# The modulation vector as row sums on VectorE, over a matrix laid out transposed

## What is computed

```python
c_act = jax.nn.silu(c)                       # (1, 2048)
mod = c_act @ w_ada + b_ada                  # w_ada (2048, 6144)
shift, scale, gate = jnp.split(mod, 3, axis=-1)
h = rms_norm(x, g) * (1.0 + scale[:, None]) + shift[:, None]
...
return x + gate[:, None] * out
```

## Time and profile before

| | |
|---|---|
| median of three runs | 2671.77 us (2671.35 to 2673.11) |
| the profiled execution | 2669.51 us |
| its span, first to last instruction | 2668.2 us |
| mean granted clock of TensorE over the span | 0.998 of full |
| busy: TensorE, VectorE, ScalarE, GpSimd | 99%, 48%, 33%, 3% |
| HBM read, mean rate | 297.80 MB, 115 GB/s over the span |

### The profile page before, as it was taken

One profiled execution on the slowest core, in us unless ns is written; L12 is line 12 of the kernel. 1 busy time (PEld: TensorE's weight loads), 2 busy tenths in 40 slices (PEclk: granted clock), 3 DMA queues, 4 the chain that ended last, 5 costly groups with the idle time before them and its releaser, 6 DMA issues.

```text
span 2668.2 us, 28964 instructions
## 1 busy us (share of the span) xinstructions
PE 2631.1 (99%) x11830; PEld 2135.4 (80%) x11830; DVE 1276.1 (48%) x1806; ACT 888.8 (33%) x1232; POOL 91.9 (3%) x75
## 2 busy tenths in 40 slices
PE   8999999999999999999999999999999999999998
PEld 6888888888888888888888887778866777777888
DVE  7546634447434555655542263563343334443425
ACT  5633324333323222222232352332232333433323
POOL 4000000000000000000000011100000000000000
PEclk9999999999999999999999999999999999999999
DMA  5322233222233666666443223234312322222424
GB/s 180 103 80 71 79 87 99 84 79 71 87 95 123 209 209 209 201 204 211 142 158 110 88 87 107 83 100 162 95 54 65 95 71 79 72 72 86 160 100 150
DMA packets 159364, 308.07 MB, mean 115 GB/s; under 512 B 10944, under 2 KB 15296, under 8 KB 158208
## 3 DMA queue, kind: packets, MB, share of 16 engines
q1 hardware_dynamic: 158432, 304.65, 35.8%
q0 software_dynamic: 224, 1.15, 0.1%
q10 hardware_dynamic: 576, 0.43, 0.1%
HBM read 297.80 MB, written 8.39 MB: 115 GB/s over the span
## 4 chain that ended last, share of the span: by engine, by line
PE 93%; DVE 3%; issue 2%; ACT 1%; DMA 0%; POOL 0%; SPq 0%; ACTq 0%; DVEq 0%; POOLq 0%
PE bank L329 84%; PE bank L669 2%; PE bank L1205 1%; PE bank L1101 1%; PE bank L1179 1%; PE bank L385 1%; PE bank L688 1%; DVE WL L361 1%; DVE XL L454 1%; PE bank L1194 1%; PE bank L1090 1%; DMA X<-in_xT 0%; PE bank L956 0%; ACT WH L347 0%; DVE Y L1916 0%
## 5 line engine op out<-in xcount | busy, mean ns | idle before, releaser
L329 PE MATMUL bank<-XH,WH 128*128 128x512 f32 (+1 forms) x2880 | 1150.5, 399 | 19.0 <-DVE XL L454 10.6
L329 PE MATMUL bank<-XH,WL 128*128 128x512 f32 (+1 forms) x2880 | 1111.2, 386 | 3.8 <-DVE WL L361 3.8
L329 PE MATMUL bank<-XL,WH 128*128 128x512 f32 (+1 forms) x2880 | 1108.9, 385 | 0.0
L361 DVE TENSOR_TENSOR WL<-RAW,WH 128x1024 fp32r<-128x1024 f32 x444 | 547.7, 1236 | 960.7 <-ACT WH L347 959.9
L347 ACT CAST WH<-RAW 128x1024 fp32r<-128x1024 f32 x444 | 464.2, 1047 | 1202.8 <-PE bank L329 1197.1
L329 PEld LDWEIGHTS bank<-XH,WH 128*128 128x128 f32 x2880 | 542.5, 188 | 139.9 <-issue 31.8
L329 PEld LDWEIGHTS bank<-XL,WH 128*128 128x128 f32 x2880 | 542.8, 188 | 118.4 <-issue 15.8
L329 PEld LDWEIGHTS bank<-XH,WL 128*128 128x128 f32 x2880 | 542.0, 188 | 116.8 <-DVE WL L361 5.5
L329 PE MATMUL bank<-WH,XH 128*128 128x512 f32 x384 | 154.2, 401 | 0.0
L329 PE MATMUL bank<-WL,XH 128*128 128x512 f32 x384 | 149.6, 390 | 0.0
L329 PE MATMUL bank<-WH,XL 128*128 128x512 f32 x384 | 149.4, 389 | 0.0
(11 more groups left out here) (241 smaller groups left out, 1679.8 us busy)
## 6 DMA issues: line engine op xcount, KB each, us to landing
RAW<-in_w_in SPq DMA_DIRECT2D x304, 512.0 KB, 3.6
AST<-in_w_ada SPq DMA_DIRECT2D x192, 256.0 KB, 3.7
RAW<-in_w_out SPq DMA_DIRECT2D x40, 512.0 KB, 3.5
RAW<-in_w_o SPq DMA_DIRECT2D x32, 512.0 KB, 3.6
RAW<-in_w_gate SPq DMA_DIRECT2D x32, 512.0 KB, 3.6
RAW<-in_w_a SPq DMA_DIRECT2D x16, 512.0 KB, 4.1
RAW<-in_w_b SPq DMA_DIRECT2D x16, 512.0 KB, 4.1
XT<-in_xT SPq DMA_DIRECT2D x4, 1024.0 KB, 6.6
```

Source lines behind the costliest of these rows:

```text
L329: ins = nc.tensor.matmul(bank[b][:, cols], l, r[:, cols], start=first, stop=final)
L361: nc.vector.tensor_tensor(WL[:, m % NSPL], RAW[:, m % NRAW], WH[:, m % NSPL].bitcast(F32), ALU.subtract).then_inc(lo.sem, lo.step(m))
```

## The change

The matrix is handed over in another layout, made on the host: instead of 2048 rows (inputs) by 6144 columns (outputs) it is cut into 192 tiles of 128 outputs by 512 inputs, each contiguous. Tile n has the quarter q = n // 48 of the inputs and the block t = n % 48 of the outputs. Now an output lies on a partition, and its sum runs along the row. `c` comes as a row of 2048 numbers, of which 512 at a time are loaded to all 128 partitions (`load_c`, 256 KB in SBUF) into CB, two buffers; ScalarE makes its sigmoid in SGT (which lies where MASK was, used by the recurrence only), VectorE the product, silu(c), in CB.

For each tile VectorE then runs one `tensor_tensor_reduce`: the product of the tile and CB, written over the tile, and its row sums in one column of PART. After 192 tiles four small adds of 128x48 put together the four quarters and the bias into MOD. TensorE has no part in it; no PSUM bank is taken. The turns, their pace, the three tile buffers and the place in the order stay. The rows of c for quarter q + 1 are loaded at tile 8 of quarter q, their sigmoid is made at tile 24, their product at tile 32. The first is loaded ahead of the first three tiles.

```diff
@@ -264,7 +264,7 @@
     raw = [Signal(nc, f"raw{i}", 16) for i in range(NRAW)]
     ld = {name: Signal(nc, f"load_{name}", 16) for name in
           ("vec", "log", "idn", "msk", "x0", "x1", "x3", "x6", "x10", "xt0", "xt1", "xt2", "xt3", "p", "cst",
-           "ada0", "ada1", "ada2", "x3_0", "x3_1", "x3_2", "x3_3")}
+           "ada0", "ada1", "ada2", "c", "x3_0", "x3_1", "x3_2", "x3_3")}
     stored = Signal(nc, "out_stored", 16)
     spilled = Signal(nc, "x3_spilled", 16)
 
@@ -827,8 +827,9 @@
     M = sb("M", [16, 512], F32, W0 + 49152)
     SG = sb("SG", [4, 512], F32, W0 + 81920)
     AST = sb("AST", [3, 512], F32, W0 + 90112)
-    ACC = sb("ACC", [2, 512], F32, W0 + 96256)
-    CA = SM[:, 48:64]
+    CB = sb("CB", [2, 512], F32, W0 + 96256)
+    PART = sb("PART", [192], F32, W0 + 100352)
+    SGT = sb("SGT", [512], F32, C0 + 1024)
 
     def conv_dve(half):
         for i in range(4):
@@ -890,74 +891,72 @@
     O_MADE = [(dve, ("silu", ("og", j // 4), j % 4)) for j in range(8)]
     M_MADE = [(dve, ("m", j)) for j in range(16)]
 
+    def load_c(q):
+        nc.sync.dma_start(CB[:, q % 2], crow[:, 512 * q:512 * q + 512].partition_broadcast(128)
+                          ).then_inc(ld["c"].sem, ld["c"].step(q))
+
+    def load_ada(n):
+        s = ld[f"ada{n % 3}"]
+        nc.sync.dma_start(AST[:, n % 3], w_ada[n]).then_inc(s.sem, s.step(n))
+
     def ada_sp():
+        Y.wait_ge(xlo, (yield xlo, ("ya", 7)))
+        Y.wait_ge(dve, (yield dve, ("silu", ("og", 1), 3)))
+        load_c(0)
         for n in range(3):
-            if n == 0:
-                Y.wait_ge(xlo, (yield xlo, ("ya", 7)))
-                Y.wait_ge(dve, (yield dve, ("silu", ("og", 1), 3)))
             load_ada(n)
         yield
         for n in range(192):
+            q, t = divmod(n, 48)
             if n + 3 < 192:
                 Y.wait_ge(dve, (yield dve, ("ada", n)))
                 load_ada(n + 3)
-            yield
-
-    def load_ada(n):
-        c, k = divmod(n, 16)
-        s = ld[f"ada{n % 3}"]
-        nc.sync.dma_start(AST[:, n % 3], w_ada[k * 128:k * 128 + 128, 512 * c:512 * c + 512]
-                          ).then_inc(s.sem, s.step(n))
+            if t == 8 and q < 3:
+                load_c(q + 1)
+            yield
+
+    def c_act(q):
+        A.wait_ge(ld["c"], (yield ld["c"], q))
+        if q:
+            A.wait_ge(dve, (yield dve, ("c", q - 1)))
+        else:
+            A.wait_ge(dve, (yield dve, ("silu", ("og", 1), 3)))
+        A.use(SIG)
+        nc.scalar.activation(SGT[:, :], CB[:, q % 2], ACT.Sigmoid).then_inc(act.sem, act.step(("c", q)))
 
     def ada_act():
-        A.wait_ge(ld["vec"], (yield ld["vec"], 0))
-        A.use(SIG)
-        nc.scalar.activation(CA, vall("c"), ACT.Sigmoid).then_inc(act.sem, act.step("ca"))
-        yield
-        yield from idle(192)
+        yield from c_act(0)
+        yield
+        for n in range(192):
+            q, t = divmod(n, 48)
+            if t == 24 and q < 3:
+                yield from c_act(q + 1)
+            yield
+
+    def c_dve(q):
+        V.wait_ge(act, (yield act, ("c", q)))
+        nc.vector.tensor_tensor(CB[:, q % 2], CB[:, q % 2], SGT[:, :], ALU.mult).then_inc(dve.sem, dve.step(("c", q)))
 
     def ada_dve():
-        V.wait_ge(act, (yield act, "ca"))
-        nc.vector.tensor_tensor(CA, CA, vall("c"), ALU.mult).then_inc(dve.sem, dve.step("ca"))
+        yield from c_dve(0)
         yield
         for n in range(192):
-            c, k = divmod(n, 16)
-            s, u = n % 3, c % 2
-            V.wait_ge(ld[f"ada{s}"], (yield ld[f"ada{s}"], n))
-            if k == 0:
-                V.wait_ge(dve, (yield dve, "ca"))
-                if c > 1:
-                    V.wait_ge(side, (yield side, ("ada", c - 2)))
-                elif c == 0:
-                    V.wait_ge(dve, (yield dve, ("silu", ("og", 1), 3)))
-                nc.vector.tensor_scalar(ACC[:, u], AST[:, s], CA[:, 0:1], None, ALU.mult
-                                        ).then_inc(dve.sem, dve.step(("ada", n)))
-            else:
-                V.wait_ge(dve, (yield dve, ("ada", n - 1)))
-                nc.vector.scalar_tensor_tensor(out=ACC[:, u], in0=AST[:, s], scalar=CA[:, k:k + 1],
-                                               in1=ACC[:, u], op0=ALU.mult, op1=ALU.add
-                                               ).then_inc(dve.sem, dve.step(("ada", n)))
-            yield
-            if k == 15:
-                V.wait_ge(side, (yield side, ("ada", c)))
-                nc.vector.tensor_tensor(MOD[:, 4 * c:4 * c + 4], bank[banks["ada", c]][:, 0:4],
-                                        vall("b_ada")[:, 4 * c:4 * c + 4], ALU.add
-                                        ).then_inc(dve.sem, dve.step(("mod", c)))
-
-    def ada_pe():
-        yield
-        for n in range(192):
-            c, k = divmod(n, 16)
-            if k == 15:
-                b, was = special_bank(("ada", c), dve, ("mod", c))
-                T.wait_ge(was[0], (yield was))
-                T.wait_ge(dve, (yield dve, ("ada", n)))
-                for j in range(4):
-                    ins = nc.tensor.matmul(b[:, j:j + 1], ACC[:, c % 2, 128 * j:128 * j + 128], ONES[:, 0:1],
-                                           start=True, stop=True)
-                    if j == 3:
-                        ins.then_inc(side.sem, side.step(("ada", c)))
-            yield
+            q, t = divmod(n, 48)
+            if t == 32 and q < 3:
+                yield from c_dve(q + 1)
+            V.wait_ge(ld[f"ada{n % 3}"], (yield ld[f"ada{n % 3}"], n))
+            V.wait_ge(dve, (yield dve, ("c", q)))
+            nc.vector.tensor_tensor_reduce(AST[:, n % 3], AST[:, n % 3], CB[:, q % 2], 1.0, 0.0, ALU.mult, ALU.add,
+                                           PART[:, n:n + 1]).then_inc(dve.sem, dve.step(("ada", n)))
+            yield
+        V.wait_ge(dve, (yield dve, ("ada", 191)))
+        nc.vector.tensor_tensor(MOD[:, :], PART[:, 0:48], PART[:, 48:96], ALU.add).then_inc(dve.sem, dve.step("mod1"))
+        for q in (2, 3):
+            V.wait_ge(dve, (yield dve, f"mod{q - 1}"))
+            nc.vector.tensor_tensor(MOD[:, :], MOD[:, :], PART[:, 48 * q:48 * q + 48], ALU.add
+                                    ).then_inc(dve.sem, dve.step(f"mod{q}"))
+        V.wait_ge(dve, (yield dve, "mod3"))
+        nc.vector.tensor_tensor(MOD[:, :], MOD[:, :], vall("b_ada"), ALU.add).then_inc(dve.sem, dve.step("mod"))
 
     XT = sb("XT", [16, 512], F32, W0 + 49152)
     X1 = sb("X1", [16, 512], F32, W0)
@@ -1007,7 +1006,7 @@
                 yield
 
     def feed_h2_act():
-        A.wait_ge(dve, (yield dve, ("mod", 11)))
+        A.wait_ge(dve, (yield dve, "mod"))
         for k in range(16):
             A.wait_ge(dve, (yield dve, ("h2n", k)))
             A.wait_ge(dense, (yield dense, (("gate", 3), 3)))
@@ -1352,7 +1351,6 @@
         for g in range(4):
             yield from pe_dense(("ga", g), XH, XL, "h")
             if g == 0:
-                turns.specials.append(ada_pe())
                 turns.pace = 1.2
             yield from pe_dense(("wa", g), YH, YL, "ya")
         for g in range(4):
@@ -1871,7 +1869,7 @@
                     nc.vector.tensor_scalar(WG[:, i], WG[:, i], EPS, None, ALU.add
                                             ).then_inc(dve.sem, dve.step(*(["wg"] if i == 3 else [])))
         yield from rsqrt_dve("r_12", 1.0 / D, NN[:, 0], R12, NN[:, 2], eps=EPS * EPS)
-        V.wait_ge(dve, (yield dve, ("mod", 11)))
+        V.wait_ge(dve, (yield dve, "mod"))
         nc.vector.tensor_scalar(GG, MOD[:, 16:32], 1.0, None, ALU.add).then_inc(dve.sem, dve.step("gg0"))
         V.wait_ge(dve, (yield dve, "gg0"))
         nc.vector.tensor_tensor(GG, GG, vall("ng"), ALU.mult).then_inc(dve.sem, dve.step("gg"))
@@ -2082,7 +2080,8 @@
         "xT": np.ascontiguousarray(i["x"][0].T), "pT": np.ascontiguousarray(i["p"][0, 0].T),
         "vec": vec, "logits": logits, "cst": cst, "masks": masks, "ident": ident,
         "w_in": i["w_in"][0], "w_a": i["w_a_out"][0], "w_b": i["w_b_out"][0], "w_o": i["w_o"][0],
-        "w_gate": i["w_ple_gate"][0], "w_proj": i["w_ple_proj"][0], "w_ada": i["w_ada_2"][0],
+        "w_gate": i["w_ple_gate"][0], "w_proj": i["w_ple_proj"][0], "w_ada": i["w_ada_2"][0].reshape(4, 512, 48, 128).transpose(0, 2, 3, 1).reshape(192, 128, 512),
+        "crow": i["c_2"].reshape(1, D),
         "w_in2": i["w_in_2"][0], "w_out2": i["w_out_2"][0],
     }
     arrays = {f"in_{k}": np.ascontiguousarray(v) for k, v in arrays.items()}
```

More of the change, by code:

```diff
@@ L217, in build @@
 def build(nc, xT, pT, vec, logits, cst, masks, ident, w_in, w_a, w_b, w_o, w_gate, w_proj,
-          w_ada, w_in2, w_out2, out):
+          w_ada, crow, w_in2, w_out2, out):
     weights = {"w_in": w_in, "w_a": w_a, "w_b": w_b, "w_o": w_o, "w_gate": w_gate, "w_proj": w_proj,
@@ L919, in ada_dve @@
-    def ada_dve():
-        V.wait_ge(act, (yield act, "ca"))
```

(18 more changed lines are left out.)

## The result

The changed kernel takes 2658.42 us (median of four runs, 2657.58 to 2659.36) against 2671.86 before: a ratio of 0.9949, 95% interval 0.9938 to 0.9961, so 13.4 us (10.4 to 16.6) less. Forecast were 2659.5 us and 12.2 us less. The profiled execution took 2657.58, with a span of 2656.1; the sum had 2656.0.

A forecast was written before the change was run, and what follows sets the result against it. TensorE's dense products were taken to bound the stage; removing twelve small-product groups (11 x 0.90 + 2.34 = 12.2 us), with VectorE's work costing nothing, gave a 2656.0 us span and a 2659.5 us forecast, range 2656 to 2665.

The forecast's parts named there:

- The bound: Stage making the modulation vector, 840 to 1360 us: time is a sum over TensorE's work, 97.4% dense products of line 329.
- The price of a group: Twelve groups of small products on TensorE: eleven push dense products apart by about 0.90 us, the sixth 2.34; 12.2 removed.
- The price of a row: Each of 192 fused products with row sums on VectorE: 0.77 us at most, 149 us in all, off TensorE's path.
- The upper bound of a row: Dearest 128x512 two-source operation, line 454: 1432 ns, 1.51 us with the read, still under the cover's end at 1.65.
- Two fp32 sources: VectorE's row sums: doubt whether two fp32 SBUF sources run slower; line 937's 749 ns shows no penalty, skill's rule gives 1.24 us.
- The start of the stage: First c lands between 852.7 and 856.1 us, VectorE's split ends between 856.6 and 858.7, due 863.3; nothing on the path.
- The cover of 10 us for a landing: First load of c: over 4 us of cover before TensorE needs the split, for a landing up to some 10 us.
- Landing of the tiles: Matrix tiles, now contiguous with the same 2 KB per partition: landing may only get shorter, nobody on the path waits.
- Banks: PSUM banks 6 and 7 not taken in the stage: no new wait, bound zero to one eviction's 0.6 us.
- The second: Rival: no change, small products filled gaps and TensorE regains only about 2 us; 2667 to 2671 us, chance 0.03.
- the third rival: Slower: VectorE becomes the stage's bound from 1.65 us a row; 2688 us at 1.8 us a row, chance 0.03.
- the first: Rival: rows at 1.2 to 1.5 us make VectorE's splits late, eating up to half the gain; 2661 to 2666, chance 0.06.

## Why the prediction was right

- **The bound.** Right: a stage that is a sum over TensorE's instructions gives back what is taken out of the sum. Both ways of taking the products out gave 463.0 us, and putting them back gave 474.3.
- **The price of a group.** The sum had 11 x 0.90 + 2.34 = 12.2 us; the stage shrank by 12.3. The stand in the sixth group measured 1.5 us by itself, against 1.44 worked out. The step that mattered was to read the price from how far apart the dense products are pushed and not from a general figure for a small product. Here busy time, 11.5 us, would have come out nearly as well, by luck: it puts 0.7 us too much on the twelve groups (10.8) and misses the stand of 1.4.
- **The price of a row.** Mis-sized, on the safe side. I added 692 and 82 ns to 0.77 us. Two rows that don't wait for each other start 0.61 us apart (0.73 where the second waits, in the kernel with three rows): the read starts before the product has ended, and the next product with it. The timeline of the changed kernel:

```profile
866.13 0.69 DVE L949 CUSTOM_DVE_ANT_0 AST<-AST,CB 128x512 f32<-128x512 f32 x1
866.74 0.09 DVE L949 DVE_READ_ACCUMULATOR2_ANT PART<- 128x1 f32 x1
866.74 0.69 DVE L949 CUSTOM_DVE_ANT_0 AST<-AST,CB 128x512 f32<-128x512 f32 x1
```

  The multiply-adds before took 1.60 us for two, since each read what the last had written. So VectorE was busy for 253.7 us in the window (56%), not 274.5 (62%). No time hung on it.
- **The upper bound of a row.** Misread, and that it did no harm was luck. 1432 ns is the mean of two levels of line 454; half of its instructions took 1779 ns or more. Before:

```profile
L454 DVE SCALAR_TENSOR_TENSOR XL<-X,V,XH x16: 739/1779/1790, 9.7 to 40.1; 128x512 fp32r<-128x512 f32 x16
```

  With the read that makes up to 1.87 us, above the 1.65 at which the cover ends and not below it: 192 x 0.22 = 42 us over. The argument that even the upper bound costs nothing fails by that. Why it wasn't needed: the dear ones lie where GpSimd adds (mostly 17.5 to 39.0 us), as the prediction says, and GpSimd does nothing from 850 to 1305 us. The rows took 682 to 694 ns. That GpSimd's adds are the cause is argued from the times alone.
- **Two fp32 sources.** The doubt behind the bounds is settled: 687 ns with two fp32 sources in SBUF, 692 with the float16 table. The halved rate of the Trainium skill ("Vector Engine (DVE) Microarchitecture Reference", section "Points that are easy to get wrong") isn't seen in this operation. (The estimate by that rule adds up to 1.22 us from its own numbers, not 1.24.)
- **The start of the stage.** Within its bounds. c landed at 855.3, not at the 853.8 that I took; VectorE's split ended at 857.8 (forecast 856.6 to 858.7); TensorE, working on from 852.65, never noticed. The changed kernel, to the earlier trace rows:

```profile
855.33 0.63 ACT L925 ACTIVATE SGT<-CB 128x512 f32<-128x512 f32 x1 [0.94 <-DMA CB<-in_crow]
```

```profile
855.99 0.69 DVE L938 TENSOR_TENSOR CB<-CB,SGT 128x512 f32<-128x512 f32 x1 [6.22 <-ACT SGT L925]
856.60 1.22 DVE L361 TENSOR_TENSOR WL<-RAW,WH 128x1024 fp32r<-128x1024 f32 x1
```

- **The cover of 10 us for a landing** was right as a length of time, as far as a late sigmoid shows it: TensorE would have wanted the split at 864.25, and it ended at 857.8, so c could have landed some 11 us after its issue at 850.29. What I expected beyond the cover in the run with c late, a loss of one for one, was wrong: the clock falls behind the wait.
- **Landing of the tiles.** "May only get shorter" was wrong: the median went from 3.7 to 4.1 us, and to 4.2 with strided tiles, so the layout isn't what sets it. It follows the distance of the rows on VectorE: 2.9 us with three rows a tile, 3.4 with two, 3.7 with the multiply-adds of before, 3.9 with the same multiply-adds where TensorE doesn't hold them up, 4.1 in the changed kernel. The faster VectorE frees buffers, the closer tiles are asked for. That this is the cause is argued from the order of these numbers, not shown by itself.
- **Banks.** No wait for a bank appeared in the changed kernel's stage, as worked out.
- **Rivals.** The second and third are refuted as written: the groups did push the dense products apart, and VectorE was far from its bound, for which the runs with more rows agree with the third rival's 1.65 us. For the first, even 1.35 us a tile took nothing back.

## What to carry to other kernels

In a stage where one engine's instructions stand end to end in the chain, price what you take out by how far it pushes its neighbours apart, and what you put on another engine by that engine's idle time in the stage divided by the count of operations (here 1.65 us a row; 1.35 cost nothing, 2.08 cost 79.4 us, and nothing between them was run). When a bound is taken from a row of the profile, look at its shortest and longest and not only at its mean. The small products here were paid by the pass, 0.11 us each with a load of weights of its own, whether they summed ACC or multiplied a constant; the same sum laid along the row cost nothing on a VectorE that was idle for 44% of the stage. When several things are changed at once, the kernel before with only the suspected cost removed is the cheapest way to see which of them made the time.

## What was unexpected about the hardware

- A product with row sum on VectorE and its accumulator read overlap: 0.69 and 0.08 us by duration, 0.61 from one to the next.
- A stand of 4.2 us cost TensorE another 1.55, at a granted clock of 0.55 for the seven products behind it. The stand of 1.2 us at the sixth group before had left the dense products behind it 0.23 apart. In the kernel with three rows, six stands of 5.5 to 7.6 us cost 14.3 us more in this way, and the clock is 0.96 on average over the stage.
- One row of 2 KB repeated to all partitions landed in 4.3 to 5.0 us, about as long as a tile of 256 KB (2.5 to 5.6 us, median 4.1).
- Line 454, a product and a difference of 128x512 on VectorE, took 0.74 us in some instructions and 1.79 in others; the long ones lie beside GpSimd's adds.
